# Prompt tokens and sample tokens apart: where the pages stream, and which tokens share a weight chunk

## The reference

```
def reference(...):
    for l in range(DEPTH):                      # DEPTH 2, D_MODEL 1024
        hp, hs = rms_norm(yp, ...), rms_norm(ys, ...)
        if l % 2 == 0:
            mp, ... = even_mixer(hp, pos_p, s0=0, None, None, ...)
            k_past = cache_k[e][page_table]     # 8 samples x 32 pages x (128 tokens x 512)
            v_past = cache_v[e][page_table]
            ms, ... = even_mixer(hs, pos_s, state_ret[e], k_past, v_past, ...)
        else:
            mp, ms = chunk_gmlp(hp, ...), chunk_gmlp(hs, ...)
        yp = ffn(yp + mp, ...); ys = ffn(ys + ms, ...)

def even_mixer(h, ...):                         # h @ w_in: 1024 -> 4608
    ro = head_group_norm(retention(rq, rk, rv, s0)) * silu(rg)
    do = rms_norm(diff_attn(dq, k_all, v_all, ...), sub_g)
    return concat([ro, do]) @ w_out             # 1536 -> 1024

def chunk_gmlp(h, ...):                         # 1024 -> 2 x 3072
    u, v = split(gelu(h @ w_in), 2)
    s = einsum('gts,bnsgc->bntgc', tri(w_s), layer_norm(v)) + b_s
    return (u * s) @ w_out                      # 3072 -> 1024

def ffn(y, g, w_up, w_down):                    # 1024 -> 4096 -> 1024
    return y + square(relu(rms_norm(y, g) @ w_up)) @ w_down
```

## Time and profile before

| | us |
|---|---|
| runs | 2046.92, 2042.52, 2046.82 |
| median | 2046.82 |
| profiled execution | 2045.41 |
| its span, first to last instruction | 2043.6 |

### The profile page before, as it was taken

The page is one execution under the profiler, slowest core; times in us unless marked ns, Lnnn a source line. Parts: engine busy times, 40 slices in busy tenths (PEclk is TensorE's granted clock), DMA queues, the critical chain, the costliest instruction groups (busy, mean ns, idle before and its releaser), DMA issues.

```text
span 2043.6 us, 35465 instructions
## 1 busy us (share of the span) xinstructions
PE 1882.8 (92%) x14237; PEld 1683.9 (82%) x14237; DVE 909.9 (45%) x1155; ACT 568.6 (28%) x915; POOL 636.0 (31%) x510
## 2 busy tenths in 40 slices
PE   4967888899998799999999999979999999999998
PEld 4855555555554599999999899879999999999997
DVE  2577676665552544332333423393323443323331
ACT  4422333322231232221222232303313333212221
POOL 1388554777740013300431100023304224102400
PEclk8988898999996799999999999979999999999999
DMA  6258686899997223332323322202322232332221
GB/s 206 92 165 270 232 258 207 315 335 356 337 320 243 94 83 94 99 92 90 92 93 93 95 63 82 67 10 74 101 86 92 89 98 83 104 91 86 92 93 63
DMA packets 218268, 287.95 MB, mean 141 GB/s; under 512 B 12977, under 2 KB 149762, under 8 KB 217858
## 3 DMA queue, kind: packets, MB, share of 16 engines
q1 hardware_dynamic: 215306, 281.95, 41.8%
q10 hardware_dynamic: 2208, 2.75, 0.4%
q0 software_dynamic: 624, 1.44, 0.4%
HBM read 274.89 MB, written 11.21 MB: 140 GB/s over the span
## 4 chain that ended last, share of the span: by engine, by line
PE 81%; DVE 8%; DMA 3%; ACT 3%; SPq 2%; issue 2%; POOL 1%; ACTq 0%; DVEq 0%
PE ps L1639 18%; PE ps L1641 18%; PE ps L1640 18%; PE ps L1449 6%; PE ps L1451 5%; PE ps L1450 5%; PE ps L1495 4%; DMA vbuf<-in_cache_v 2%; DVE Sc L1138 1%; PE ps L1540 1%; POOL kbuf L633 1%; PE ps L1706 1%; PE ps L1422 1%; PE ps L1527 1%; PE ps L1519 1%
## 5 line engine op out<-in xcount | busy, mean ns | idle before, releaser
L488 DVE TENSOR_TENSOR w_lo<-raw,w_hi 128x1024 fp32r<-128x1024 f32 x238 | 334.7, 1414 | 498.2 <-ACT w_hi L481 497.1
L1639 PE MATMUL ps<-xg_hi,w_hi 128*128 128x260 f32 x1408 | 398.6, 283 | 0.5 <-DVE sTs L1409 0.5
L1641 PE MATMUL ps<-xg_hi,w_lo 128*128 128x260 f32 x1408 | 398.4, 283 | 0.0
L1640 PE MATMUL ps<-xg_lo,w_hi 128*128 128x260 f32 x1408 | 397.3, 282 | 0.0
L633 POOL TENSOR_TENSOR kbuf<-kbuf,Qb 128x512 f32<-128x512 f32 x256 | 344.4, 1373 | 141.0 <-DMA kbuf<-in_cache_k 140.9
L481 ACT ACTIVATE w_hi<-raw 128x1024 fp32r<-128x1024 f32 x248 | 259.1, 1054 | 460.9 <-PE ps L1641 413.0
L1449 PE MATMUL ps<-w_hi,xg_hi 128*128 128x256 f32 (+1 forms) x1200 | 352.4, 294 | 21.8 <-DVE w_lo L488 9.4
L1450 PE MATMUL ps<-w_lo,xg_hi 128*128 128x256 f32 (+1 forms) x1200 | 344.6, 287 | 0.0
L1451 PE MATMUL ps<-w_hi,xg_lo 128*128 128x256 f32 (+1 forms) x1200 | 344.2, 287 | 0.0
L1641 PE MATMUL ps<-h_hi,w_lo 128*128 128x260 f32 x1024 | 289.3, 283 | 0.0
L1639 PE MATMUL ps<-h_hi,w_hi 128*128 128x260 f32 x1024 | 289.1, 282 | 0.0
(11 more groups left out here) (274 smaller groups left out, 2543.0 us busy)
## 6 DMA issues: line engine op xcount, KB each, us to landing
kbuf<-in_cache_k SPq DMA_DIRECT2D x256, 256.0 KB, 4.5
vbuf<-in_cache_v SPq DMA_DIRECT2D x256, 256.0 KB, 4.9
raw<-in_w_ffn_up SPq DMA_DIRECT2D x64, 512.0 KB, 3.8
raw<-in_w_ffn_down SPq DMA_DIRECT2D x64, 512.0 KB, 3.5
raw<-in_w_in_odd SPq DMA_DIRECT2D x48, 512.0 KB, 3.8
raw<-in_w_in_even SPq DMA_DIRECT2D x36, 512.0 KB, 5.5
raw<-in_w_out_odd SPq DMA_DIRECT2D x24, 512.0 KB, 3.6
raw<-in_w_out_even SPq DMA_DIRECT2D x12, 512.0 KB, 3.6
```

The costliest lines, as they stand in the source:

```text
L488: dve.tensor_tensor(w_lo[:, c.slot], raw[:, c.slot % 2], w_hi[:, c.slot].bitcast(F32), ALU.subtract).then_inc(lo_made, 1)
L1639: pe.matmul(out, wh, xh, start=kk == 0, stop=False, skip_group_check=True)
L1640: pe.matmul(out, wh, xl, start=False, stop=False, skip_group_check=True)
L1641: mm_ = pe.matmul(out, wl, xh, start=False, stop=kk == KC * groups - 1, skip_group_check=True)
```

## The change

The samples are taken out of the wide matrices of layer 0, of oe and of the gMLP, and follow on their own, with the weights read a second time.

- In the in-projection the tile of the samples comes first in a macro (`TILES`, `NT` is the samples'), ahead even of the first prompt tile for macros 0 and 1. Tokens are loaded after the first chunks, two chunks go to a buffer of their own (`early`). DVE makes all low parts. The attention units stand 1.5 tiles apart. The state updates go by head (`sL`, `sM`, `sU`, `sO`) between tiles of macros 12 to 17, and 8 slots (`TAIL`) hold the samples' outputs and the mixes.
- The page stream and all of the samples' later work are one list of 337 ticks (`sample_ticks`). `plan` deals them out over 276 slots: 98 of in-projection and tail, 76 chunks of oe to dn01, 48 tiles of v, 6 of the gate stage, 48 chunks of u and oo. `PACE` says how many ticks a slot gets. By slot 97, 76 K and 32 V pages are through; the last K page is in slot 154, the last V page in slot 167.
- `prompts` takes the place of `wide` in these phases: 512 prompt tokens as one matmul of 512 columns, 24 matmuls a chunk. v has four tiles a macro. u and oo go in three thirds.
- The samples' products (`sW`): 148 chunks of the same weights in fp32, loaded by SP into a ring of four (`ring_in`, from slot 174), each 4 matmuls of 8 rows by 256 columns in the four row groups, then copied (`sE`) and folded (`sF`). They add 77.6 MB of loads. sW 0 to 37 stand in v, 38 to 55 in the gate stage, 56 to 147 in slots 228 to 257 of u and oo. For up10 to dn11 prompt and samples are together again, as before.

PE runs `background(j)` behind each slot; it waits there for `v_loaded` and `ring_loaded` with the next chunk's matmuls behind it.

```diff
-            + [("v", 2, N_V)] + [(f"{k}{h}", g, m) for h in range(2) for k, g, m in (("u", 2, 6), ("oo", 3, 4))]
+            + [("v", 2, N_V)] + [(f"{k}{h}", g, m) for h in range(3) for k, g, m in (("u", 2, 4), ("oo", 2, 4))]
...
 SPS = NPAGES // PER
-LAG = SPS + 4
+LAG = SPS + 6
...
-LO_SWITCH = 5
+FIRST_STEP = 4
+TAIL = 8
+RING = 4
...
+def _tiles():
+
+    seq = [(0, NT), (1, NT)]
+    for m in range(N_IN):
+        seq += [(m, NT)] * (m > 1) + [(m, t) for t in range(NT)]
+    return seq
...
-    if s < NS and at == SPS - 1:
-        out.append(("soft1", s))
-    if 1 <= s < NS - 1 and at == 4:
+    if 1 <= s <= NS and 2 <= at < 7:
+        out.append((("soft1", "maxT", "maxB", "soft2", "soft3")[at - 2], s - 1))
+    if 1 <= s < NS - 1 and at == 8:
         out.append(("qb", s + 1))
-    if 1 <= s <= NS and at < 4:
-        out.append((("maxT", "maxB", "soft2", "soft3")[at], s - 1))
...
-        line = [(11 + 2 * h, t) for t in range(NT + 1)]
-        after[12 + 2 * h, 0].append(("rS", h))
+        j = AT[11 + 2 * h, NT]
         for n in range(NT):
-            after[12 + 2 * h, n + 1].append(("rC", h, n))
-        for i, at in enumerate(line):
...
-    step = 0
-    for m in range(3, N_IN):
-        for t in range(NT + 1):
-            for n in range(2):
-                if step < STEPS and (n == 0 or m > 4):
-                    after[m, t] += kv_step(step)
-                    step += 1
-                if n == 0:
-                    after[m, t] += middle[m, t]
-            after[m, t] += late[m, t]
-
...
+            first[j + 1 + n].append(("rB", h, n))
+            first[j + n].append(("rA", h, n))
+        j = AT[12, NT] + 8 * h
+        first[j - 1].append(("sL", h))
+        first[j - 1].append(("sM", h))
+        for p in range(NS // 2):
+            first[j + p].append(("sU", h, p))
+        first[j + NS // 2].append(("sO", h))
...
+    ticks = list(SAMPLE)
+    pace, after = 0.0, []
+    for j in range(slots):
+        kind = "in" if j < NTILE + TAIL else SLOT_KIND[j - NTILE - TAIL]
+        if j >= FIRST_STEP:
+            pace += PACE[kind]
+        now = []
+        while pace >= 1.0 and ticks:
+            now.append(ticks.pop(0))
+            pace -= 1.0
+        if j < NTILE + TAIL:
+            now = first[j] + (now[0] if now else []) + middle[j] + [s for tick in now[1:] for s in tick] + late[j]
+        else:
+            now = [s for tick in now for s in tick]
+        after.append(now)
...
+    out, first = [], 0
+    for name, groups, pairs in (("oe", 3, 2), ("up", 2, 8), ("dn", 8, 2), ("v", 2, 6), ("u", 2, 6), ("oo", 6, 2)):
+        for q in range(pairs):
+            out.append((name, q, [(first + i, i // groups, i % groups, groups) for i in range(2 * groups)]))
+            first += 2 * groups
+    return out
...
+    for p, (name, q, chunks) in enumerate(GEMM):
+        for n, *_ in chunks:
+            tick([("sW", n)])
+        ticks[-1].append(("sE", p))
+        later(2, ("sF", p))
+        if name == "u":
...
+SLOT_KIND = (["oe"] * 12 + ["up"] * 16 + ["dn"] * 16 + ["up"] * 16 + ["dn"] * 16 + ["v"] * (NT * N_V) + ["gate"] * 6
+             + ["u"] * 48)
+B0 = NTILE + TAIL
+V0 = B0 + 76
+G0 = V0 + NT * N_V
+U0 = G0 + 6
+PACE = {"in": 0.4, "oe": 1.6, "up": 1.55, "dn": 1.7, "v": 1.0, "gate": 3.0, "u": 3.4}
 AFTER = plan()
...
+def slot_of(c):
+
+    return B0 + c - 2 * N_IN if c < PHASES["v"][0] else U0 + c - PHASES["u0"][0]
...
-            for c in range(AHEAD + 2):
+            for c in range(2):
                 in_chunk(c)
-
+            sp.dma_start(xst[:, :, 0:D // 2], x_rows[:, :, 0:D // 2]).then_inc(x_loaded, 16)
+            for c in range(2, 4):
+                sp.dma_start(early[:, c - 2], chunk_rows(w_in_even[0], c % 2, IN_COLS[c // 2])).then_inc(early_loaded[c - 2], 16)
...
+            def ring_in(n):
+
+                if n < len(LOADS):
+                    name, q, mm, g = LOADS[n]
+                    w, at = sample_weights[name]
+                    wait(sp, s_multiplied, n + 1 - RING)
+                    sp.dma_start(ring[:, n % RING], chunk_rows(w, g, at + CW * (2 * q + mm))).then_inc(ring_loaded[n % RING], 16)
...
+                elif kind == "sB":
+                    sp.wait_ge(k_scored, NG)
+                    sp.wait_ge(v_used, NG)
+                    for n in range(RING - 1):
+                        ring_in(n)
+                elif kind == "sW":
+                    ring_in(step[1] + RING - 1)
...
+            for j in range(B0):
+                m, t = TILES[j] if j < NTILE else (N_IN, 0)
+                if m < N_IN and t == 0 and m > 0:
+                    in_chunk(2 * m + AHEAD + 1)
+                if m < N_IN and t == 2:
+                    in_chunk(2 * m + AHEAD + 2)
+                for step in AFTER[j]:
+                    sp_step(step)
...
+                elif kind == "sW":
+                    name, q, mm, g = LOADS[i]
+                    p = [k for k, end in enumerate(PAIR_END) if i < end][0]
...
+                    pe.wait_ge(ring_loaded[i % RING], 16 * (i // RING + 1))
+                    for k in range(KC):
+                        row = (P // QUAD) * k
+                        last = pe.matmul(ps[row:row + NS, PV[p % 2], CW * mm:CW * mm + CW], src[:, KC * g + k, :],
+                                         ring[:, i % RING, k, :], start=g == 0, stop=g == last_group, skip_group_check=True)
+                    last.then_inc(s_multiplied, 1)
...
+            def background(j):
+
+                for step in AFTER[j]:
+                    pe_step(step)
...
+            def prompts(name, high, low, ready, counts, e=None):
+
+                c0, groups, macros = PHASES[name]
+                for m in range(macros):
+                    wait(pe, acc_read, BLOCK0[name] + 2 * m - 2)
+                    for g in range(groups):
+                        c = Chunk(0, 0, 0, c0 + groups * m + g)
+                        pe.wait_ge(lo_made, c.n + 1)
+                        pe.wait_ge(ready, counts[g])
+                        for blk in range(2):
+                            out, cols = sums(m, blk), slice(P * blk, P * blk + P)
+                            for k in range(KC):
+                                kk = KC * g + k
+                                wh, wl, xh, xl = w_hi[:, c.slot, k, cols], w_lo[:, c.slot, k, cols], high(kk), low(kk)
+                                pe.matmul(out, wh, xh, start=kk == 0, stop=False, skip_group_check=True)
+                                pe.matmul(out, wh, xl, start=False, stop=False, skip_group_check=True)
+                                last = pe.matmul(out, wl, xh, start=False, stop=kk == KC * groups - 1, skip_group_check=True)
+                        last.then_inc(chunk_multiplied, 1)
+                        if e is not None and m == 0 and g == 0:
+                            squares(e)
+                        background(slot_of(c.n))
+                    if e is not None and m == 0:
+                        pe.wait_ge(root_made, e)
+
...
+
+            c0 = PHASES["v"][0]
+            for mac in range(N_V):
+                cs = [Chunk(0, 0, 0, c0 + 2 * mac + g) for g in range(2)]
+                pe.wait_ge(lo_made, cs[1].n + 1)
                 for t in range(NT):
-                    src = ro[:, t, P * b:P * b + P] if b < 8 else doN[:, t, P * (b - 8):P * (b - 8) + P]
-                    last = turn(ps[:, PAIR[b % 2], P * t:P * t + P], src, P)
...
-            def wide(name, per, src_hi, src_lo, ready, counts, e=None, first=1):
+                    if mac == 0:
+                        pe.wait_ge(xg_lo_made, KD * 3)
...
+                    natural(cs, t, ACC[t], xb_hi, xb_lo, NT - 1)
+                    if mac == 0 and t == 1:
+                        squares(2)
+                    background(V0 + NT * mac + t)
```

1607 lines of the change are left out of this document (982 added, 625 removed).

## The result

The changed kernel takes **2025.95 us** (median of five, 2023.16 to 2031.54), the kernel before 2042.52 beside it: a ratio of 0.9923, 95% interval [0.9904, 0.9943]. It is 0.8% faster, where 3.8% were forecast (1970 us). The time lies in the range; the direction was right; the size was off by a factor of almost five.

What follows compares the result with a forecast made beforehand. DMA and DVE were taken to bound the in-projection's page streaming, PE the wide matrices. Stages summed 459 + 530 + 172 + 61 + 361 + 371 + 15 = 1969 us of span, forecast 1970; range 1875 to 2050.

Steps and rivals of the forecast that it cites:

- What bounds the kernel now: Whole kernel: pages stream where DMA and DVE are the bound; PE alone bounds the wide matrices, with DMA two thirds idle.
- The in-projection: In-projection and tail: fall from 704 to 459 us, as 29 + 95 + 130 + 175 + 30.
- The attention on PE, "some 33": Macros 6 to 10: the prompt's attention takes some 33 us of PE beside 71 for its tiles.
- DVE's 112: Macros 6 to 10: DVE's 162 us less 55 of page reductions plus 5 for lows gives 112, within 130 for the stage.
- 18 for waits between exp, mix and transpose: Macros 6 to 10: 18 us of waits added to DVE's time, which no faster stream removes, giving 130.
- The clock: In-projection: tiles priced at 2.83 us; clock at 0.95 or above from 100 us on, since PE's gaps close.
- The tail, 30: Tail after the in-projection: 83 us before, 30 after; twelve mixes 14.3 us, the samples' output chain about as long.
- oe to dn01: 76 chunks: 444 to 530 us; 57 page slots at 7.2 us (410) and 19 more at 6.3 (120).
- v, gate, u and oo: Later stages: v 175 to 172 us, gate 59 to 61, u and oo 277 to 361 with 30 sample slots at 8.8.
- Rival 2: PE's in-order stops on V quads or sample chunks not yet landed make it about 2110 to 2150 us; chance 0.11.
- Rival 1: All at PE's pace: page slots 6.5 us, sample slots 7.8, no waits in macros 6 to 17, about 1880 us; chance 0.20.
- Rival 3: In-projection stays bound by chains rope to transpose and exp to mix to transpose: 60 us less gained, 2030; chance 0.07.

Runs made afterwards that it cites:

- all_three: Changed kernel with snew and key masks moved, attention units respaced and cut to one key block, no page steps in the in-projection: 2016.36 us, ratio 0.9851 to before.
- halves: Changed kernel with each 512-column matmul of oe, up0, dn0, u and oo made as two of 256 columns: 2037.33 us, ratio 0.9976 to before.
- ring_quarter: Changed kernel with only a quarter of each re-read weight chunk loaded from the fifth on: 2020.59 us, ratio 0.9904 to before.
- late_snew: Changed kernel with snew put behind the second prompt tile of macro 5 instead of the first of macro 3: 2014.61 us, ratio 0.9849 to before.

## Why the prediction was wrong

**What bounds the kernel now: right, with a gap.** It was right that pages streamed beside DMA-bound and DVE-bound tiles, and that the wide stages had room. The step from "DMA and DVE are busy there" to "take them away and PE's work is left" was the fault: for macros 6 to 10 DVE was 162 busy of 229 us and PE 192 in the earlier trace rows, at clock 0.91. PE's 192 us were the larger number and I passed over it. The sum for this stage went by DVE, 112 us and 18 of waits. DVE measured 74.2 us and bounds nothing; PE's 147.9 busy and 34.0 idle are the 181.9.

**The in-projection: the term that failed.** 459 was the sum, 547 the start of oe.
- *The attention on PE, "some 33".* It had no row, though the trace of before has 57 us for it. 58 us are measured in the changed kernel, and cutting its blocks from 2.5 to one took 30.8 us away. With 58, PE's 71 + 58 would have passed DVE's 112, and with the 18 of waits the stage would have stood at 147 instead of 130: 17 of the +52. The other 35 are 15 for tiles at the lower clock, 16 for more idle time and 4 for small products.
- *DVE's 112.* The sum took 55 us of reductions out and left the rest at its price beside a busy POOL. That rest became cheaper as well: POOL is busy 28.5 of 181.9 us there, before 137.9 of 229. The same product of the attention on DVE, before (170 to 399 us) and after (146 to 328 us):
```profile
L1185 DVE SCALAR_TENSOR_TENSOR pq<-pq,tiny 128x384 f32<-128x384 f32 x4 | 6.4, 1608 | 0.1
L1640 DVE SCALAR_TENSOR_TENSOR pq<-pq,tiny 128x384 f32<-128x384 f32 x4 | 2.5, 619 | 0.1
```
- *"18 for waits between exp, mix and transpose", and 10 in macros 0 to 5.* PE was idle for 34.0 and 22.2 us there. 13.3 of the 22.2 is one wait for DVE at snew, which the change had moved from macro 5 to macro 3, where DVE had the samples' and the prompt's rotations queued. The kernel before had a wait of this kind already, longer than all that the sum allows the stage:
```profile
PE ps L1477 <- DVE tiny L1131: 15.7, 1, 15.7
```
  I named neither the queue nor the waiter. Moving the step brought oe 8 us forward.
- *The clock.* The sum had every tile at 2.83 us, the upper level. The clock stayed at 0.90, 0.87 and 0.95 in the three parts; the 25 tiles of macros 6 to 10 took 85.9 us instead of 71. "PE's gaps close" was assumed under what would show it, and didn't happen. Filled waits gave 12 us in the changed kernel.
- *Pages.* In macros 11 to 17 I priced quads but no more. Without any page 29 us went, where the sum has 6 for quads and 13 on DVE, the latter only in macros 6 to 10.
- *The tail, 30.* Measured 30.7; state updates "some 35" and quads 6 lie within macros 11 to 17, 13 us off as a whole.

all_three takes attention blocks, two waits and the pages away and lands at 470.5, within 12 us of the sum. So the terms for attention, waits and pages account for most of the 88 us. It doesn't bear out the sum's reasoning: the stage that missed most was put down to DVE, and it is PE's own row of tiles, small products and waits, at the clock that these leave.

**oe to dn01: right in sum.** 527.1 against 530. The page slots were 401.6 / 57 = 7.05 us, forecast 7.2, with DMA at 0.89. A quad with landed pages cost 0.98 us again:
```profile
580.18 1.04 PE L1918 MATMUL ps<-vbuf,Sc 128*8 128x512 f32 x8
581.15 0.50 PE L2122 MATMUL ps<-mb_hi,w_hi 128*128 128x512 f32 x1
```
But the pitch at 512 columns is 233 ns, not 224.4: two rows at almost the same width (256 and 260) can't tell a fixed part from a proportional one, and agreed with both. Most chunks of u and oo with nothing of the samples behind them took 5.49 to 5.61 us instead of 5.39. By this pitch the wider form is worth 711 - 2976 x 0.233, some 17 us, instead of 43 (an estimate; halves measured 11 against two of 256 columns). The extra of 7.2 over PE's 6.5 covered that error, so the 530 is in part luck. The figure of the Trainium skill (TensorE: Matmul & The Clock Gate, "Wait — 56ns, not 53.3ns?"), 215.8 ns, is still further off.

**v, gate, u and oo: right mechanism, priced too high.** A sample chunk in v pushed the next matmul back by 0.55 us, the forecast's number:
```profile
1202.50 0.62 PE L1996 MATMUL ps<-ring,cst 128*8 128x256 f32 x8
1203.05 0.38 PE L1872 MATMUL ps<-w_hi,xb_hi 128*128 128x256 f32 x1
```
The 30 slots with sample chunks took 8.06 us in the mean, PE's work, not 8.8; there was no stop to pay for, as ring_quarter shows. The gate stage shrank to 43.7 us where 61 were put; with four tiles a macro and no samples' rows its chain is shorter, which I only argue.

**The rivals.** Rival 2 (stops on data that hasn't landed) is refuted: 48 of the 56 quads in oe to dn01 pushed the next matmul back by 0.97 or 0.98 us, all 56 by 1.10 in the mean, and the 92 sample chunks in u and oo by 0.55. Rival 1 (all at PE's pace) holds for u and oo, and fails in the in-projection. Rival 3, with 0.07, was nearest: the in-projection stays bound by its own work and chains, with 29 of the 88 us due to pages. It had the size, 60 us, too low; its time of 2030 came within 4 us because gate, u and oo gave 33 us back, which is luck. Its evidence was clock 0.86 and 36 us of idle PE in macros 0 to 5, and it got a tenth of the weight of the main case. ("Much of it ahead of the first page" was misread: 8 of the 36 us lie before POOL's first K product at 94 us.) In a stage where PE idles and the clock is down, the waits should have been listed and costed first.

The port pair that DVE and POOL share by the Trainium skill (SBUF — State Buffer, "Who interferes with whom") was weighed at +23 us. The trace agrees that they block each other, and the trace of before already did (1608 ns for 619 above). In the page slots (547 to 950 us) the two that have both inputs in SBUF are dearer than my 1.41 and 1.37, and the reduction, with one input, is not:
```profile
L649 DVE TENSOR_TENSOR w_lo<-raw,w_hi 128x1024 fp32r<-128x1024 f32 x57 | 98.9, 1735 | 98.5 <-ACT w_hi L642 98.4
L858 POOL TENSOR_TENSOR kbuf<-kbuf,Qb 128x512 f32<-128x512 f32 x176 | 261.5, 1519 | 42.3 <-DMA kbuf<-in_cache_k 42.0
L1476 DVE TENSOR_REDUCE Sc<-kbuf 128x8 f32<-128x512 f32 x182 | 116.3, 675 | 20.7 <-POOL kbuf L858 20.6
```
In the whole trace of the changed kernel a `w_lo` with no POOL product beside it took 1.23 us in the median, one with a POOL product beside it 1.86. It shows where POOL is nearly full: in up00 it is busy 109.5 of 117.1 us, and a slot took 7.32 us where POOL had been put at 6.6. The 8.0 us that the prediction got from the rule were not reached, and the 13 page slots of up01 took 6.65. So the extra in 7.2 covered this error as well.

## What to carry to other kernels

Before a stream is moved out of a stage, add up what each engine has to do in order there without it, from rows, and list the waits that remain: the stage won't fall to the next engine's busy time, but to its chain of small steps, at the clock that such a chain leaves. Where TensorE waits a microsecond or two for another engine again and again, idle matmuls in the wait can pay, if they are shorter than the wait. A cost per column needs two widths that differ.

## What the runs showed of the hardware

- A matmul of 512 columns (fp32r) starts 233 ns after the one before it (172 in 40 us of the changed kernel), 19 ns over its columns at 2.4 GHz; 256 and 260 columns have 11. Two of 256 take 235.6.
- TensorE's clock: with 8 waits of 2.4 us in macros 6 to 10 it was 0.84 to 0.87 over 182 to 188 us (four profiles); with idle matmuls in them 0.95 over 168 us, and with late_snew besides 0.90 over 180; with the same matmuls elsewhere 0.91 over 189. The Trainium skill (TensorE: Matmul & The Clock Gate, "What's actually happening") says that the clock is set by how busy PE was of late; these runs agree in direction. What they add is that idle matmuls in a wait cost almost nothing (1.8 us for 12.2) and gave 15.4 us back.
- DVE and POOL block each other when both of DVE's inputs are in SBUF: 619 ns became 1608 for a 128x384 product, 1.23 us became 1.86 for `w_lo`. A reduction of one input took 676 ns in the median with and without POOL beside it.
- Executions of one kernel differ: 12 of the changed kernel ran from 2015.7 to 2034.9 us, and late_snew had two of 2009 to 2010 and two of 2019 to 2022. What makes the difference is not shown.
